# Router logits with stationary weights in two column groups, and 28 cached pages issued from GpSimd's queue

## What is computed

```python
att = mla_sample_attention(q_nope, q_rope, concat([past_ckv, ckv]), concat([past_krope, krope]), ...)  # 8 samples, 16 cached pages each
h1 = layer_norm(DN_ALPHA * x + einsum('blm,md->bld', y, w_out), ln1_g, ln1_b)
g_logits = (xf @ w_group).astype(f32) + b_group          # xf = h1, 1024 -> 4
e_logits = (xf @ w_expert).astype(f32) + b_expert        # 1024 -> 32
# best group, the two best of its 8 experts, their weights; 32 experts of 1024 -> 256 -> 1024
ple = einsum('blp,pd->bld', p, w_pe) * sigmoid(einsum('bld,de->ble', h1, w_pg))
out = layer_norm(DN_ALPHA * h1 + moe + ple, ln2_g, ln2_b)
```

## Time and profile before

| | us |
|---|---|
| median of 3 runs | 2628.98 |
| the 3 runs | 2628.98, 2629.95, 2623.26 |
| the profiled execution, own time | 2624.26 |
| its span, first to last instruction | 2622.4 |
| PE busy | 2365.0 (90%) |
| DVE busy | 1150.1 (44%) |
| ACT busy | 700.4 (27%) |
| POOL busy | 275.1 (10%) |

### The profile page before, as it was taken

The page is one execution under the profiler, slowest core; times in us unless marked ns, Lnnn a source line. Parts: engine busy times, 40 slices in busy tenths (PEclk is TensorE's granted clock), DMA queues, the critical chain, the costliest instruction groups (busy, mean ns, idle before and its releaser), DMA issues. The chain is left out here.

```text
span 2622.4 us, 40200 instructions
## 1 busy us (share of the span) xinstructions
PE 2365.0 (90%) x15128; PEld 1223.3 (47%) x15128; DVE 1150.1 (44%) x2864; ACT 700.4 (27%) x1424; POOL 275.1 (10%) x405
## 2 busy tenths in 40 slices
PE   7999979867998999999599999788789899999977
PEld 3555545555554443333255555455645544333323
DVE  3444446644765122322345554566457531222225
ACT  2555444423211000000044555344222110000011
POOL 1111009200000200000000000570000020000001
PEclk9999979988998999999799999899889899999988
DMA  9476147441312549999553322663332252799956
GB/s 331 168 249 231 58 114 206 108 134 61 146 45 109 193 167 386 419 420 416 217 195 108 100 66 60 174 182 79 120 126 88 104 200 84 306 420 420 420 237 259
DMA packets 244252, 519.80 MB, mean 198 GB/s; under 512 B 67927, under 2 KB 151967, under 8 KB 218697
## 3 DMA queue, kind: packets, MB, share of 16 engines
q1 hardware_dynamic: 199656, 393.42, 41.7%
q0 software_dynamic: 23984, 82.60, 8.7%
q10 hardware_dynamic: 20416, 41.16, 4.1%
HBM read 386.05 MB, written 131.04 MB: 197 GB/s over the span
## 5 line engine op out<-in xcount | busy, mean ns | idle before, releaser
L493 PE MATMUL pj_zp<-pj_w,pj_xT 128*128 128x512 f32 (+1 forms) x1280 | 504.2, 541 | 3.6 <-DMA pj_w<-in_w_in 2.8
L2153 PE MATMUL op_bank<-ex_wgu,ex_xT 128*32 128x512 f32 x3072 | 344.9, 601 | 11.7 <-DMA ex_wgu<-in_e_up 5.9
L493 PEld LDWEIGHTS pj_zp<-pj_w,pj_xT 128*128 128x128 f32 x1280 | 225.3, 192 | 202.1 <-issue 193.9
L2041 PE MATMUL op_bank<-op_wout,op_hT 128*128 128x512 f32 x512 | 234.3, 617 | 1.5 <-issue 1.5
L2084 PE MATMUL op_bank<-op_wpg,op_hT 128*128 128x512 f32 x512 | 226.9, 602 | 0.0
L2153 PEld LDWEIGHTS op_bank<-ex_wgu,ex_xT 128*32 128x32 f32 x3072 | 98.1, 111 | 221.4 <-issue 210.3
L2173 PE MATMUL op_bank<-ex_wd,ex_hT 128*32 128x512 f32 x1536 | 174.7, 595 | 1.5 <-DVE ex_y L2612 1.5
L2617 DVE TENSOR_TENSOR ex_h<-ex_sil,op_bank 128x256 f32<-128x256 f32 x48 | 20.2, 421 | 342.0 <-ACT ex_sil L2314 342.0
L2314 ACT ACTIVATE ex_sil<-op_bank 128x256 f32<-128x256 f32 x48 | 18.4, 384 | 558.6 <-PE op_bank L2153 558.6
L2041 PEld LDWEIGHTS op_bank<-op_wout,op_hT 128*128 128x128 f32 x512 | 100.6, 200 | 123.3 <-issue 120.9
L2084 PEld LDWEIGHTS op_bank<-op_wpg,op_hT 128*128 128x128 f32 x512 | 98.9, 194 | 123.4 <-issue 123.2
(11 more groups left out here) (430 smaller groups left out, 3342.4 us busy)
## 6 DMA issues: line engine op xcount, KB each, us to landing
ex_wgu<-in_e_gate SPq DMA_DIRECT2D x64, 1024.0 KB, 11.3
ex_wgu<-in_e_up SPq DMA_DIRECT2D x64, 1024.0 KB, 14.1
ex_wd<-in_e_down SPq DMA_DIRECT2D x64, 1024.0 KB, 15.1
h<-scratch_XR SPq DMA_DIRECT2D x48, 512.0 KB, 15.0
scratch_YR<-ex_y ACTq DMA_DIRECT2D x48, 512.0 KB, 8.1
scratch_XR<-pj_zero POOLq DMA_DIRECT2D x41, 512.0 KB, 8.2
pj_w<-in_w_in SPq DMA_DIRECT2D x8, 2048.0 KB, 17.6
pc_ckv<-in_cache_ckv SPq DMA_DIRECT2D x256, 64.0 KB, 1.9
```

Of the source, the lines that this page charges most:

```text
L493: last = pe.matmul(zp[c % ZB][:, 0:cn], xT[:, t % 2, k, :], w[:, k, c0:c0 + cn], start=(k == 0), stop=(k == KC - 1), skip_group_check=True)
L2041: last = pe.matmul(op[n][:, :], hT[:, t, c, :], wout[:, c, n * 512:(n + 1) * 512], start=(c == 0), stop=(c == KC - 1))
L2153: last = pe.matmul(gu[q % 2][part], xT[:, q % 2, c, part], wgu[s][:, :, c, :], start=(c == 0), stop=(c == KC - 1), skip_group_check=True)
```

## The change

Two parts. Of the 48 pages that SP issues last in the prompt attention, 28 go to the end of POOL's stream in the same stage, with a semaphore of their own. And the logits are made with the router's weights stationary (36 columns) and the turned h1 moving (128 columns): chunks of the contraction with an even number are summed in rows 0 to 35 of a PSUM bank, the odd ones in rows 64 to 99, DVE copies both into `lT`, and one matmul with the constant `fold` (two identities, one above the other) sums the halves and turns them back. This last step runs one tile later, the p of tile 0 is turned after the gates of tile 0, and the turn back of the ninth tile stands between the halves of those gates.

```diff
     COUNTS = (24, DECB * PAGES - 24)
+    LATE = 28
 
...
 
-    def load(self, eng, d, layer, first, count, phase):
+    def load(self, eng, d, layer, first, count, phase, sem=None):
 
             for p, page in enumerate(pages, p0):
-                eng.dma_start(self.ckv(p), d["cache_ckv"][layer, ds(page, 1)].rearrange("g k n -> (g k) n")).then_inc(self.pages_loaded[phase], 16)
-                eng.dma_start(self.kr(p, 1), d["cache_krope"][layer, ds(page, 1)].rearrange("g k n -> (g k) n")).then_inc(self.pages_loaded[phase], 16)
+                eng.dma_start(self.ckv(p), d["cache_ckv"][layer, ds(page, 1)].rearrange("g k n -> (g k) n")).then_inc(sem or self.pages_loaded[phase], 16)
+                eng.dma_start(self.kr(p, 1), d["cache_krope"][layer, ds(page, 1)].rearrange("g k n -> (g k) n")).then_inc(sem or self.pages_loaded[phase], 16)
 
...
                 sample.load(sp, d, layer)
-                cache.load(sp, d, layer, cache.COUNTS[0] + 56, cache.COUNTS[1] - 56, 1)
+                cache.load(sp, d, layer, cache.COUNTS[0] + 56, cache.COUNTS[1] - 56 - cache.LATE, 1)
 
...
                 pool.dma_start(of_layer(d["conv_s"], layer), u[0:DECB, 1:3, :]).then_inc(cv_state, 16)
+                cache.load(pool, d, layer, DECB * PAGES - cache.LATE, cache.LATE, 1, d["sw"]["late_pages"])
                 for s in range(2):
...
                 last.then_inc(prep, 1)
-                for n, loaded in zip(cache.COUNTS, cache.pages_loaded):
-                    pe.wait_ge(loaded, 32 * n)
+                pe.wait_ge(cache.pages_loaded[0], 32 * cache.COUNTS[0])
+                pe.wait_ge(cache.pages_loaded[1], 32 * (cache.COUNTS[1] - cache.LATE))
+                pe.wait_ge(d["sw"]["late_pages"], 32 * cache.LATE * (layer + 1))
                 turned(0)
...
         hold = ph.sb("op_hold", [1, 1])
+        lT = ph.sb("op_lT", [64 + NR, P])
+        fold = ph.sb("op_fold", [64 + NR, NR])
         rb = ph.sb("ro_b", [P, NR])
...
         typ, tph = (four(0), four(1)), (four(4), four(5))
-        op, lp = (bank[2], bank[3]), bank[6]
+        op, lp, lb = (bank[2], bank[3]), bank[6], bank[7]
         gpair = ((bank[4], bank[5]), (bank[0], bank[1]))
...
         x_ready, var_ready, xd_done, h1_ready = (ph.sem(n) for n in ("x_ready", "var_ready", "xd_done", "h1_ready"))
-        th_done, th_dve, th_act, l_done, l_ready = (ph.sem(n) for n in ("th_done", "th_dve", "th_act", "l_done", "l_ready"))
+        th_done, th_dve, th_act, l_done, fold_steps, lT_ready, lb_done, l_ready = (
+            ph.sem(n) for n in ("th_done", "th_dve", "th_act", "l_done", "fold_steps", "lT_ready", "lb_done", "l_ready"))
         pt_done, pT_ready, g_done, e_done = (ph.sem(n) for n in ("pt_done", "pT_ready", "g_done", "e_done"))
...
                     if t:
+                        pe.wait_ge(lT_ready, t)
+                    for c in range(0, KC, 2):
+                        for i in range(2):
+                            last = pe.matmul(lp[64 * i:64 * i + NR, 0:P], wr[:, c + i, :], hT[:, t, c + i, :], start=(c == 0), stop=(c == KC - 2),
+                                             skip_group_check=True)
+                    last.then_inc(l_done, 1)
+
+                def logits_turned(t):
+                    pe.wait_ge(lT_ready, t + 1)
+                    if t:
                         pe.wait_ge(l_ready, t)
-                    for c in range(KC):
-                        last = pe.matmul(lp[:, 0:NR], hT[:, t, c, :], wr[:, c, :], start=(c == 0), stop=(c == KC - 1))
-                    last.then_inc(l_done, 1)
+                    else:
+                        pe.wait_ge(fold_steps, 4)
+                    pe.matmul(lb[:, 0:NR], lT[:, :], fold[:, :], start=True, stop=True).then_inc(lb_done, 1)
 
...
                     for n in range(2):
+                        if t == 0 and n == 1:
+                            logits_turned(NT - 1)
                         for c in range(KC):
...
                         y_turned(t + 1)
+                    if t >= 2:
+                        logits_turned(t - 2)
                     if t:
                         logits(t - 1)
-                p_turned(0)
                 h_turned(NT - 1)
+                logits_turned(NT - 2)
                 logits(NT - 1)
                     gates(t)
+                    if t == 0:
+                        pe.wait_ge(l_ready, NT)
+                        p_turned(0)
                     if t == 1:
...
 
-                p_copied(0)
                 act.wait_ge(r_steps, 2)
                 act.activation(ge[:, :, :], gd[:, :, :], ACT.Exp).then_inc(r_act, 1)
+                p_copied(0)
                 act.wait_ge(r_steps, 26)
...
 
+                def logits_copied(t):
+                    dve.wait_ge(l_done, t + 1)
+                    if t:
+                        dve.wait_ge(lb_done, t)
+                    dve.tensor_copy(lT[0:NR, :], lp[0:NR, 0:P])
+                    dve.tensor_copy(lT[64:64 + NR, :], lp[64:64 + NR, 0:P]).then_inc(lT_ready, 1)
+
                 def route_in(t):
-                    dve.wait_ge(l_done, t + 1)
+                    dve.wait_ge(lb_done, t + 1)
                     dve.wait_ge(r_loaded, 16 * 2)
-                    TT(L[:, t, :], lp[:, 0:NR], rb[:, :], ALU.add).then_inc(l_ready, 1)
+                    TT(L[:, t, :], lb[:, 0:NR], rb[:, :], ALU.add).then_inc(l_ready, 1)
 
                 step_parts = sample_step()
+                dve.memset(lT[:, :], 0.0).then_inc(fold_steps, 1)
+                dve.memset(fold[:, :], 0.0).then_inc(fold_steps, 1)
+                dve.wait_ge(fold_steps, 2)
+                for i in range(2):
+                    own = slice(64 * i, 64 * i + NR)
+                    dve.tensor_copy(fold[own, :], ident[own, own]).then_inc(fold_steps, 1)
                 dve.wait_ge(out.mixg_loaded, 32)
...
                         h_copied(t - 1)
+                    if t >= 2:
+                        route_in(t - 2)
                     if t == 0:
                     if t:
-                        route_in(t - 1)
+                        logits_copied(t - 1)
                     if t + 2 < NT:
                 h_copied(NT - 1)
+                route_in(NT - 2)
+                logits_copied(NT - 1)
                 route_in(NT - 1)
...
         d["sw"] = {n: ctx.enter_context(nc.semaphore(f"sw_{n}")) for n in
-                   ("zero_stored", "cv_w", "cv_in0", "cv_in1", "cv_out0", "cv_out1", "cv_state", "scattered", "rows_in")}
+                   ("zero_stored", "cv_w", "cv_in0", "cv_in1", "cv_out0", "cv_out1", "cv_state", "late_pages", "scattered", "rows_in")}
         with Phase(nc) as ph:
```

## The result

The changed kernel takes **2584.65 us**, the median of four executions (2583.80 to 2590.71), against 2628.49 for the kernel before (four, 2623.26 to 2629.95): a ratio of 0.985, 95% interval 0.9835 to 0.9864, or 36 to 43 us. I had forecast 2602 us with a range of 2590 to 2618. The direction was right. My sum was 24.9 us; by the ratio the gain is 39.4 us, by the two medians 43.8. The profiled executions differ by 39.2 us (2624.26 and 2585.06).

What follows compares the result with a forecast made beforehand. TensorE was taken as the bound, except where it idles at the prompt attention's closing barrier for SP's queue. Part one -17.4 and part two -7.5 make -24.9 us; counted from 2626.6 that gives 2602 us, range 2590 to 2618.

Steps and rivals of the forecast that it cites:

- The rival of dear transfers on POOL: Prompt attention's pages: POOL's transfers cost as much as its indirect ones, TensorE starts at 565; 2614 us, chance 0.08.
- the slow one, POOL last at the barrier: End of prompt attention: POOL arrives last and the stage waits; at 2 us a transfer 2693 us, chance 0.04.
- the rival without overlap: Logits: the two column groups do not overlap, so logits take 1.85 us a tile; 2616 us, chance 0.12.
- 6 x 0.83 - 1.3: Middle tiles, per layer: shorter logits save 0.83 us a tile; six turns back of the logits cost 1.3 us.
- a drain at the switches of the array: Logits: switching the array between whole and grouped use costs no more than 0.1 us, held in the 0.95.
- the price of the old logits: Output projection: the old logits' 16 instructions, 736.45 to 738.23, were priced at 1.78 us a tile.
- I count nothing for the clock: Barrier ending prompt attention: no gain or loss counted for TensorE's clock as the gap shrinks from 15 to some 5 us.
- The tail: Ninth tile, logits through gates: shorter logits worth 0.8 us, added turn back and p cost more; net +0.5 us a layer.
- The delay of p: Ninth tile: p of tile 0, now after the gates, adds turn, copy and hand-overs, 1.1 us that nothing hides.
- +0.25: Last tile: DVE is on the path and the bias add now stands ahead of the norm, costing 0.25 us.
- The routing chain: DVE, ninth tile: starts after the gates' first half, 8.5 us later, ends at 835.2, 1.4 us before TensorE asks.
- its better bound: Range's 2590 end: part one -18.1, part two -14 with full overlap and switch and tail free, lower pair of executions.

Runs made afterwards that it cites:

- one group: The changed kernel with all 8 chunks of the logits in one column group, so nothing overlaps: 2597.03 us, ratio 0.9899.
- part two alone: The kernel before with only the new logits in two column groups and the turn back, all pages left on SP: 2601.85 us, ratio 0.9918.
- part one alone: The kernel before with only the 28 pages of each layer moved to POOL, logits in the old shape: 2608.92 us, ratio 0.9935.

## Why the prediction was wrong, and where it was right

**Part one was right**: 17.4 us forecast, 17.0 measured alone (13 to 22), 16.8 in the offsets. TensorE was to start at 557.7 and did at 556.83; from the store 3.4 + 1.1 us were forecast and 4.38 measured, in layer 1 4.1 + 1.1 and again 4.38. That the sum fits so well is in part luck: in layer 1 the wait behind the store shrank by 8.2 us where I had 7.4, and the store itself lost 1.5 us against the layer's start. POOL was to end near 523 and issued its last at 521.05, 0.54 us a transfer and some 1.3 us more at every table read of four pages. SP was to end at 525.5 and issued its last at 525.56. The rival of dear transfers on POOL and the slow one, POOL last at the barrier, fell with the first row. I had cited the Trainium skill (SBUF — State Buffer, SBUF: two separate sides) for VectorE copies that lock GpSimd out of descriptor writing. None of the 56 issues in layer 0 took over 0.6 us; but that page speaks of copies from SBUF to SBUF, and VectorE's copies beside these issues read PSUM (`at_tp`), so no run here tests it.

**Part two's work was about right.** Logits: 0.95 us forecast, 1.00 measured, so the rival without overlap fell too (its 1.85 is the measured 1.84 of one group). Turn back: 0.22 forecast; the next instruction follows 0.14 us behind it, and a tile got 0.21 shorter where the turn back went into the pause. For the six tiles my terms make 6 x 0.83 - 1.3 = 3.7 us a layer, and at full clock they gave 3.3. I had held a drain at the switches of the array against this, after the Trainium skill (TensorEngine Tiling (Array Packing), Tiling Modes). No row shows one of the 0.2 us that I had assumed: from the earlier trace rows I had 0.93 us for the logits in two groups and 1.85 in one, and 1.00 and 1.84 were measured, between products that use the whole array.

**The step that failed** is the price of the old logits: "1.78 us a tile". That is their own length, and it left out what they did to the instructions behind them. In five of 12 tiles, and at the outputs of the sample rows, TensorE went on at 1.2 GHz. Removing that gave 8.4 us in the tiles, and a part of the 2.4 us behind them, for which the sum had no term. "I count nothing for the clock" was argued for the barrier alone. The sign of it stood in the rows I had chosen: the earlier trace rows has eight 128x128 turns behind the logits in 1.47 us where TensorE does eight such turns in 1.05. A tile that is 1.7 us longer than its neighbour with the same 64 instructions was to be seen in any view of stretches by tile.

**The tail failed in sign**: +0.5 us forecast, -0.9 and -1.1 measured from the ninth turn on. I had the clock return at a fixed time, so that the gates pay back half of what the logits save. The stretch from the ninth turn to the count in layer 0, before and after, and TensorE's timeline of the changed kernel around it:

```profile
810.40:836.09 25.69, 24.95 (x66) 13.71 (x67) 10.44 (x46) 5.46 (x9) 0.00 (x0) 0.80 0.64 255
```

```profile
787.50:812.28 24.78, 23.38 (x72) 12.62 (x73) 11.59 (x50) 5.24 (x9) 0.00 (x0) 0.86 0.66 264
```

```profile
779.46 0.41 PE L2078 MATMUL op_bank<-op_fold,op_lT 100*128 100x36 f32 x2 [1.43 <-DVE op_lT L2477]
...
787.50 1.97 PE L2056 MATMUL op_bank<-ident,h 128*128 128x128 f32 x8 [4.52 <-DVE h L2470]
...
790.20 1.93 PE L2068 MATMUL op_bank<-op_hT,op_wr 128*36 128x128 f32 x16 [0.46 <-issue]
792.06 8.21 PE L2102 MATMUL op_bank<-op_wpg,op_hT 128*128 128x512 f32 x16
800.11 0.31 PE L2078 MATMUL op_bank<-op_fold,op_lT 100*128 100x36 f32 x2
800.25 7.11 PE L2102 MATMUL op_bank<-op_wpg,op_hT 128*128 128x512 f32 x16
807.20 0.39 PE L2085 MATMUL op_bank<-ident,op_p 128*128 128x128 f32 x2
808.53 0.48 PE L2085 MATMUL op_bank<-ident,op_p 128*128 128x128 f32 x2 [0.94 <-ACT op_pT L2304]
...
812.28 0.65 PE L2150 MATMUL op_bank<-ro_OS,ro_ones 128*128 128x288 f32 x2
```

Of 24.78 us a share of 0.14 of the clock was lost, 3.5 us; of the 25.69 us before, 0.20, 5.1 us. So the clock came back sooner after the restart than in the earlier trace rows: in stretches of 1 us it stood at 0.50 until 820.4 before, 10.0 us behind the ninth turn, and until 793.5 after, 6.0 us behind it; the logits' 1.67 us stayed won. Why it came back sooner isn't shown, and the size varies: with part two alone the same stretch took 23.35 and 24.70 us in the two layers. The delay of p is 1.33 us (807.20 to 808.53), 1.1 forecast. What I had not listed is the first row: the deferred turn back of tile 6 waits 1.43 us for DVE. By itself it cost little: with it taken back, tile 6's logits to the ninth turn took 14.02 us instead of 14.13. The ninth turn waits for DVE (4.52 us), and my "+0.25" for DVE left out that it had only 1.80 us in hand there. The routing chain was forecast 1.4 us ahead of TensorE's request; its last product on DVE ends at 810.43, 1.85 us ahead of 812.28.

The range ended at 2590 because its better bound took the work of part two at its best, with no term for the clock.

**What stays open**: which tiles fall. The same pause and the same logits let the clock fall in some tiles and not in others of one execution, and I found no row that tells them apart beforehand. That the fallen tiles are the same four in layer 0 of two kernels, and differ in layer 1, is only observed. Nor did I trace 1.5 us that layer 1's last store lost against the experts of layer 0.

## What to carry to other kernels

Price a stretch of TensorE by the distance between equal instructions of neighbouring tiles, with the granted clock of each stretch beside it: a tile that is longer with the same work has a cost that no instruction's own duration shows. Where dense work follows a pause and sparse products next to each other, try breaking the two up, by order, by shape or by work that is thrown away: each of the three ended the falls in the tiles that it changed here. Where a queue is the last at a barrier, the next to arrive bounds the gain; here it held to 1 us.

## What the runs showed that I had not expected

TensorE's clock fell at pauses well under those of the barrier (15.11 us) and of the ninth tile (3.21 us): a pause of 0.73 us with 1.78 us of 36-column products behind it, or a pause of 2.12 us with 1 us of 128-column products behind it. Neither 1.78 us of such sparse products without the pause, nor the pause with 0.89 us of them, did so in any of the 12 tiles. The Trainium skill (TensorE: Matmul & The Clock Gate, Part 1) says that the throttled state is the default and that activity releases it; the granted clock of 0.50 behind the gaps in the earlier trace rows, and its return to 1.00 while TensorE works, agree. It speaks of an idle engine, though, and in the kernel before TensorE was busy for 19.21 of 19.94 us in a tile that fell.

Discarded work paid: six more instructions a tile, 17 us less time than part one alone.
